# Attention with stationary values in column groups of the array, inside one hybrid decoder layer

## What is computed

```
attn = attend(q, k, v, qi, wi, ki).reshape(B, T, ATTN_DIM)      # 8 heads of 64, top 256 keys of each query
...
logits = jnp.einsum('bqhd,bqkhd->bqhk', q, kg) * (HEAD_DIM ** -0.5)
logits = jnp.where(valid[:, :, None, :], logits, -jnp.inf)
p = jax.nn.softmax(logits, axis=-1)
return jnp.einsum('bqhk,bqkhd->bqhd', p, vg)
...
mixed = jax.nn.sigmoid(ga) * (attn @ w_o_attn) + jax.nn.sigmoid(gc) * (conv_out @ w_o_conv)
h = x + mixed @ w_merge
```

## Time and profile before

| | us |
|---|---|
| median of 3 runs | 1750.7 (1750.21 to 1755.4) |
| span of the profiled execution | 1750.6 |
| PE busy | 1683.5 (96%) |
| DVE busy | 1242.1 (71%) |
| ACT busy | 695.0 (40%) |
| POOL busy | 881.0 (50%) |

### The profile page before, as it was taken

One profiled execution on the slowest core, in us unless ns is written; L12 is line 12 of the kernel. 1 busy time (PEld: TensorE's weight loads), 2 busy tenths in 40 slices (PEclk: granted clock), 3 DMA queues, 4 the chain that ended last, 5 costly groups with the idle time before them and its releaser, 6 DMA issues.

```text
span 1750.6 us, 31893 instructions
## 1 busy us (share of the span) xinstructions
PE 1683.5 (96%) x11519; PEld 1618.8 (92%) x11519; DVE 1242.1 (71%) x1957; ACT 695.0 (40%) x1054; POOL 881.0 (50%) x466
## 2 busy tenths in 40 slices
PE   7999999999999989999799998999999999999999
PEld 5858999999999878889799998999999999999999
DVE  5569999999899645565543378877677776655555
ACT  4755552232111377776212335434444444211110
POOL 2504762455786556664221225766666666733331
PEclk9999999999999889999999999999999999999999
DMA  5321112111776242322343312222222222622222
GB/s 197 84 70 37 36 48 86 61 49 61 267 236 207 75 140 77 87 85 85 110 135 132 143 64 80 88 75 83 72 77 79 72 94 86 231 97 96 96 77 97
DMA packets 66978, 178.32 MB, mean 102 GB/s; under 512 B 15386, under 2 KB 15514, under 8 KB 66762
## 3 DMA queue, kind: packets, MB, share of 16 engines
q1 hardware_dynamic: 56786, 140.91, 24.3%
q10 hardware_dynamic: 9392, 32.10, 4.8%
q0 software_dynamic: 720, 4.29, 0.6%
HBM read 141.79 MB, written 35.58 MB: 101 GB/s over the span
## 4 chain that ended last, share of the span: by engine, by line
PE 76%; DVE 11%; ACT 3%; POOL 3%; issue 3%; SPq 2%; DMA 1%; DVEq 0%; ACTq 0%; POOLq 0%
PE PS L667 17%; PE PS L1079 15%; PE PS L1143 11%; PE PX L1079 6%; PE PS L1002 5%; PE PS L1047 5%; PE PS L955 4%; PE PX L1143 4%; PE PS L925 2%; DVE S L2158 2%; DVE M L2156 2%; PE PX L938 2%; PE PS L983 2%; DVE LD L2138 2%; PE PS L770 1%
## 5 line engine op out<-in xcount | busy, mean ns | idle before, releaser
L667 PE MATMUL PS<-XH,WHI 128*128 128x346 f32 (+1 forms) x984 | 322.1, 327 | 5.8 <-POOL WLO L1778 4.5
L667 PE MATMUL PS<-XL,WHI 128*128 128x346 f32 (+1 forms) x984 | 318.6, 324 | 0.0
L667 PE MATMUL PS<-XH,WLO 128*128 128x346 f32 (+1 forms) x984 | 318.0, 323 | 0.0
L1778 POOL TENSOR_TENSOR WLO<-WRAW,WHI 128x1024 fp32r<-128x1024 f32 x58 | 143.4, 2472 | 296.8 <-ACT WHI L1171 296.7
L2158 DVE MATCH_REPLACE8 S<-M,S 128x1024 f32<-128x1024 f32 (+3 forms) x224 | 206.1, 927 | 0.0
L667 PEld LDWEIGHTS PS<-XH,WHI 128*128 128x128 f32 x984 | 186.9, 190 | 15.7 <-issue 8.8
L2156 DVE MAX8 M<-S 128x8 f32<-128x1024 f32 (+3 forms) x224 | 200.8, 932 | 0.4
L667 PEld LDWEIGHTS PS<-XL,WHI 128*128 128x128 f32 x984 | 187.1, 190 | 0.0
L667 PEld LDWEIGHTS PS<-XH,WLO 128*128 128x128 f32 x984 | 187.1, 190 | 0.0
L2432 DVE TENSOR_TENSOR HY<-HY,PS 128x344 f32<-128x344 f32 x198 | 100.9, 514 | 79.2 <-PE PS L1143 79.2
L1143 PE MATMUL PS<-FH,DLO 128*128 128x344 f32 x396 | 126.7, 320 | 0.0
(11 more groups left out here) (369 smaller groups left out, 4818.5 us busy)
## 6 DMA issues: line engine op xcount, KB each, us to landing
WRAW<-wtiles SPq DMA_DIRECT2D x49, 512.0 KB, 3.7
KR<-cache_k SPq DMA_DIRECT2D x64, 256.0 KB, 3.1
RING<-cache_v SPq DMA_DIRECT2D x64, 256.0 KB, 3.0
ffn_act<-TG ACTq DMA_DIRECT2D x22, 516.0 KB, 2.7
FRAW<-ffn_act SPq DMA_DIRECT2D x11, 1032.0 KB, 7.0
RAWG<-wtiles SPq DMA_DIRECT2D x22, 512.0 KB, 3.7
RAWV<-wtiles SPq DMA_DIRECT2D x22, 512.0 KB, 4.4
DRAW<-wdown SPq DMA_DIRECT2D x11, 1024.0 KB, 4.9
```

Of the source, the lines that this page charges most:

```text
L667: last = nc.tensor.matmul(PS[b][:, c, 0:n], w[b][:, kk, :], x[:, kk, t0 + c * n:t0 + (c + 1) * n], start=(kk == 0 and p == 0), stop=(kk == ...
L1778: nc.gpsimd.tensor_tensor(WLO[b][:, :, :], WRAW[b][:, :, :], WHI[b][:, :, :].bitcast(F32), ALU.subtract).then_inc(w_lo[b], 1)
```

## The change

`pv(u)` now makes the values stationary (64 columns) and the transposed probabilities moving (128 columns). Even key tiles add up on partitions 0 to 63 of `px_out`, odd ones on 64 to 127: two column groups of the array. One more matmul (`px_sum`) spreads the reciprocal row sums over partitions 64 to 127. The result has queries as columns: ACT `half(u)` copies the lower half of PSUM to `HALVES`, DVE `out(u)` adds the upper half and multiplies by the spread reciprocals into `AO`, which already has the layout of `AH`. The reciprocal moves to its own step `recip(u)`. In `attend`, ACT's order is expo(u+2), half(u-1), t_evac(u+1), and DVE's is logits(u+2), recip(u+1), out(u-1).

The decode values are multiplied in plain fp32 without casts: in units 10, 12, 14 and 16 of each head pair, sixteen matmuls (stationary 32 columns of `PZ`, moving 128 columns of `RING`) into four column groups. `value_high` and `value_low` are gone, and SP loads sixteen pages at once, behind unit 16 of the head pair before. `AH` and `AL` of the first three head pairs are made during the last one (`attention_high` on ACT at units 4, 7 and 10, the subtraction on POOL). There are no transposes at the end; the first output tile now runs q=0 before q=1, and ACT casts the weight tile (`hi(1, 21)`) ahead of the last `half`.

```
-                    last = nc.tensor.matmul(px_out[u % 2][0:ROWS[b], :], PTB[u % 2][0:w, kt, 0:ROWS[b]], v,
-                                            start=(kt == 0), stop=(kt == KT_N[b] - 1))
+                pe.wait_ge(a_rc, NU * i + u + 1)
+                    w, g = min(P, S_W[b] - kt * P), HD * (kt % 2)
+                    nc.tensor.matmul(px_out[u % 2][g:g + HD, 0:r], v, PTB[u % 2][0:w, kt, 0:r], start=(kt < 2), stop=(kt >= n - 2))
+                last = nc.tensor.matmul(px_sum[u % 2][HD:P, 0:r], SM[0:r, 36 + u:37 + u].to_broadcast([r, HD]),
+                                        CK[0:r, C_ID:C_ID + r], start=True, stop=True)
...
+                for k in range(4):
+                    for j in range(4):
+                        last = nc.tensor.matmul(px_dec[u % 2][32 * j:32 * j + 32, :], PZ[:, 4 * (i % 2) + k, heads],
+                                                RING[j // 2][:, 4 * (j % 2) + k, cols], start=(k == 0 and i % 2 == 1),
+                                                stop=(k == 3))
...
+            def half(u, i):
+                act.wait_ge(a_pv, NU * i + u + 1 + FREE)
+                nc.scalar.copy(HALVES[u % 2][HD:P, 0:r], px_out[u % 2][0:HD, 0:r]).then_inc(a_hf, 1)
...
             def out(u, i):
-                dve.wait_ge(a_exp, NU * i + u + 1)
-                nc.vector.reciprocal(SM[0:r, 36 + u:37 + u], SM[0:r, 36 + u:37 + u]).then_inc(a_rc, 1)
-                dve.wait_ge(a_pv, NU * i + u + 1 + FREE)
-                ins = nc.vector.tensor_scalar(AT[0:r, b, ds(i * P + e * HD, HD)], px_out[u % 2][0:r, :],
-                                              SM[0:r, 36 + u:37 + u], None, ALU.mult)
+                dve.wait_ge(a_hf, NU * i + u + 1)
+                if KT_N[b] > 1:
+                    nc.vector.tensor_tensor(total, total, px_out[u % 2][HD:P, 0:r], ALU.add).then_inc(a_sum, 1)
+                    dve.wait_ge(a_sum, len(SUMMED) * i + SUMMED.index(u) + 1)
+                ins = nc.vector.tensor_tensor(out, total, px_sum[u % 2][HD:P, 0:r], ALU.mult)
...
-            pe.wait_ge(a_o, 4 * NU + FREE)
-            for t in range(NB):
-                    last = nc.tensor.transpose(at_banks[t % 4][:, j * P:j * P + ROWS[t]], AT[0:ROWS[t], t, j * P:(j + 1) * P],
+            pe.wait_ge(d_o, 2)
+            for j in range(4):
+                for q in range(2):
+                    last = nc.tensor.matmul(PX[0][:, 8 * j + 4 * q:8 * j + 4 * q + 4], OD[q][:, j * P:(j + 1) * P],
```

More of the change, by code:

```diff
@@ L357, in build, with values_part @@
         KLAST_HIGH = max(g for g in range(NS * PAGES) if KSLOT[g] >= 4)
[L359 to L365, removed]
+        VALUES = (10, 12, 14, 16)
+        SPLIT = (4, 7, 10)
+        SUMMED = [x for x, (b, e) in enumerate(UNITS) if KT_N[b] > 1]
+        def values_part(u):
+            return VALUES.index(u) if u in VALUES else None
         FIRST = ("P1", "P2", "P5", "P6", "P3", "P7", "P4")
@@ L972, in decode_values @@
             def decode_values(u, i):
[L975 to L983, removed]
+                part = values_part(u)
+                if part is None:
+                    return None
+                if part == 0:
+                    for b in range(2):
+                        for h in range(2):
+                            pe.wait_ge(ring_in[b][h], 32 * PAGES + 64 * (i + 1))
+                cols, heads = slice(part * P, (part + 1) * P), slice(32 * (i // 2), 32 * (i // 2) + 32)
+                if i % 2 == 0:
+                    for j in range(4):
+                        nc.tensor.matmul(px_dec[u % 2][32 * j:32 * j + 32, :], PTN[:, heads], VT[0:LR, 8, cols], start=True, stop=False)
+                for k in range(4):
+                    for j in range(4):
+                        last = nc.tensor.matmul(px_dec[u % 2][32 * j:32 * j + 32, :], PZ[:, 4 * (i % 2) + k, heads],
+                                                RING[j // 2][:, 4 * (j % 2) + k, cols], start=(k == 0 and i % 2 == 1),
+                                                stop=(k == 3))
                 return last
@@ L995, in _, with out_chunk @@
                 attend(i, i == 3, decode_values)
+            def out_chunk(b, q, c, k0=0, k1=4):
+                xh, xl = ((AH, AL), (COH, COL))[q]
+                for kk in range(k0, k1):
+                    for p, (w, x) in enumerate(((WHI, xh), (WHI, xl), (WLO, xh))):
+                        last = nc.tensor.matmul(PS[q][:, c, 0:CW], w[b][:, 4 * q + kk, :], x[:, kk, C0 + c * CW:C0 + (c + 1) * CW],
+                                                start=(kk == 0 and p == 0), stop=(kk == 3 and p == 2))
+                return last
             def out_part(b, q):
                 for c in range(NCH):
[L999 to L1004, removed]
+                    last = out_chunk(b, q, c)
                 return last
@@ L1917, in _ @@
                 head_low(0, 0, part)
-            for q in range(3):
-                value_low(q, 0)
             attend(0, False)
@@ L2226, in attend @@
                         logits(u + 2, i)
+                    if u + 1 < NU or not last:
+                        recip(u + 1, i)
                     if u >= 1:
                         out(u - 1, i)
[L2229 removed]
+                    elif i > 0:
+                        out(NU - 1, i - 1)
+                    if i == 0 and u == 0:
                         dve.wait_ge(g_last, 16)
[L2231 to L2239 removed]
             def decode_max():
@@ L2530, in _constants @@
             ck[8 * s + h, C_NM + 16 + s] = 0.0
+    for j in range(4):
+        ck[32 * j:32 * j + 32, C_OH + j] = 1.0
+        ck[32 * j + 8 * j:32 * j + 8 * j + 8, C_OH + 4] = 1.0
     ck[0:16, C_ROWP] = 1.0
```

226 lines of the change are left out of this document (98 added, 128 removed).

## The result

The changed kernel takes 1775.2 us in the median of 4 runs (1771.03 to 1777.23), the kernel before, beside it, 1752.6 us (1750.21 to 1755.4). The ratio is 1.0134, 95% interval 1.0112 to 1.0156: 1.3% slower. I had forecast 1742 us, 0.5% faster, with a range from 1719 to 1764.

What follows compares the result with a forecast made beforehand. A closed loop over DVE and ACT, not PE, was to bound the attention: 24.7 + 1.5 + 0.4 = 26.6 us a pass, 213 + 2 + 8 = 223 us (+1); with -9 behind it about 1742 us, range 1719 to 1764.

Steps and rivals of the forecast that it cites:

- the loop I described: Attention, each unit: logits, exponential, ACT's copy, add, multiply, next logits form one closed loop, 24.7 us a pass.
- The two waits that should show it: Attention: DVE waiting for ACT's copy and ACT's exponential for DVE's maximum, together over 100 us.
- Passes are even: Attention: even and odd passes of nearly one length, 26 to 28 us.
- The mean clock: Granted clock between 612 and 836 us: 0.85 to 0.95 expected.
- The rival built on the opposite: Attention: column groups don't run side by side, PE's work is 31.1 us a pass, 1768 us; chance 0.08.
- the rest of the loop: Attention: hand-over to the exponential, copy, add, multiply and two hand-overs, 0.87 us a unit, 7.5 us a pass.
- The waits beyond it: Attention, per pass: 1.5 us ahead of block 8, 0.4 for decode adds, 1 for the clock.
- The tail: Behind the attention: even output row's matmuls done 19.9 us after the last unit's end instead of 28.9, -9 us.
- Clock: Whole attention: waiting engines get a lower clock and PE is the bound again, 1763 us at 0.72; chance 0.15.
- Shorter loop: Attention: no extra wait for block 8 and no loss by the clock, 1722 us; chance 0.17.
- A smaller gain at the end: Behind the attention: last head's copies and the convolution's casts queue on ACT, 4 of 9 us go, 1747; chance 0.10.

Runs made afterwards that it cites:

- e2: Changed kernel with a second copy of the lower half on ScalarE ahead of the real one in each of 72 units: 1785.2 us, ratio 1.0191.
- e3: Changed kernel with each unit's matmul of the sums issued three times instead of once: 1773.2 us, ratio 1.0123 to the kernel before.
- e1: Changed kernel with ScalarE's copy of unit u-1's lower half moved ahead of the exponential of unit u+2: 1729.4 us, ratio 0.9877 to the kernel before.
- e4: As e1, with the scaling of the decode results `OD` moved earlier in the last pass: 1724.6 us, ratio 0.9846 to the kernel before.

## Why the prediction was wrong

**What held.** PE was no longer the bound, and the loop I described closed. The two waits that should show it are 76.0 and 74.1 us, with 11.3 more on `AO`, well over 100. Passes are even, though at 30 to 31 us and not 26 to 28. The mean clock of 0.89 lies in 0.85 to 0.95. Column groups run side by side, as the earlier trace rows had shown: 32 records of decode values in four groups took 1.08 us, and I had taken 1.06. The rival built on the opposite fell with it. The rule on weight loads in the Trainium skill ("TensorE: Matmul & The Clock Gate", Part 3) would have had the groups one behind another, and the trace disagrees; I had passed over that the same part also measures three column tiles at 2.38 times the speed, with which the trace agrees in kind.

**What failed: the rest of the loop, taken as 0.87 us a unit.** It measures 1.10. Term by term, in the turn of the loop shown above:
- exponential's end (678.33 + 0.72) to the copy, 0.12 us where I had 0.04. The read of ACT's accumulator ends at 679.14 (678.96 + 0.18), and this copy, which writes partitions 64 to 127, starts behind it. The read alone doesn't hold the next instruction back: e2's added copy, to partitions 0 to 63, starts while it runs. The read has a row of its own in the view of the earlier trace rows, from which I took the exponential's row alone;
- copy 0.26, as in the earlier trace rows;
- start of the add to start of the multiply 0.33, and from there to the logits 0.32. I had 0.29 each and took off 0.09 for overlap. The multiply waits for the add's semaphore, and the next logits didn't overlap either.

0.23 us in the 68 units from the fifth on are 16 of the 22.9 us by which the attention missed its forecast. A term that is multiplied by 72 was put together from single durations, with the one reduction unproven.

**The waits beyond it: near.** I had 1.5 us for block 8, 0.4 for decode adds and 1 for the clock, 2.9 us a pass. Passes 2 to 7 take 30.55 us in the mean. The exponentials are 7.4 of them as forecast, the logits 10.0 for 9.8, and the loop 9.6 for 7.5 (each less one add for block 0). 3.6 us are left for 2.9. Of these 2.3 stand ahead of block 8's logits: 1.6 in passes at full clock (e3), 2.0 with a decode add, 2.6 at half clock. 0.5 stand ahead of block 0's logits. 1.1 to 1.4 stand ahead of block 4's where the clock is low at the start of a pass and PE has block 8's values and six transposes to do first, and nothing where it is full. Those two places I hadn't looked for. The clock's part, against the same places at full clock, is 4.0 us at block 8 and 5.8 at block 4, 10 us for the 8 charged: the clock was not what the forecast missed.

The account by passes, against the 222.8 us that the terms add up to: pass 1 took 27.4 us for 27.6; passes 2 to 7 took 3.0 more each than 27.6, 17.7 together; and from the start of pass 8 to the last value matmul it took 34.5 us (824.59 to 859.08) for 29.6. That is 22.4 us.

**The tail.** From the end of the last unit's matmuls (859.57) to the even row of output matmuls (880.88) it took 21.3 us for 19.9, so 7.6 us came back of 9; the table above, from the start of the last value matmul to the last output matmul, has 8.0. `OD` took 3.51 us for 3.4. Its 16 records ran at half clock (0.50), 3.58 us for 2. The 72 output matmuls behind them took 14.2 us (866.68 to 880.88) for 14.3, the low clock at their start included, where twelve took 3.60 us; twelve at full clock take 1.91 at the 0.159 us of the later ones. The wait of DVE is the one that the Trainium skill ("SBUF — State Buffer", Who interferes with whom) describes: a DVE instruction with two SBUF inputs contends with a GpSimd instruction that reads SBUF, and the order of issue decides which one is blocked. The traces agree: 2.83 us for the scaling that began behind POOL's subtraction, 0.75 for those that began ahead of it.

**The choice among cases.** With 1.10 in it the sum would have been some 17 us more, 1759: slower by 0.5%, inside the range but on the other side. What I had not asked is how firm the sum was. Before, a pass took 27.8 us, and the 9 us of the tail are 1.1 more of each; my 27.6 left 1.3 us a pass, or 0.14 us a unit, for a chain of six steps and their hand-overs. And I never worked out the edit that opens the loop, though the order of ACT was in front of me; e1's passes of 25.6 us show what was there to be had.

**The rivals.** Clock: no, at 0.89 with PE waiting, and 10 us in all. Shorter loop: no, it was longer. Groups one behind another: no. A smaller gain at the end: 7.6 of 9 us came back. That the result lies on the slower side, outside my range, is the work of the mechanism I had forecast, with a term that was too small.

## To carry to other kernels

When a change gives two engines a new hand-over inside a pipelined unit, write down each engine's order and look for a circle; if there is one, its length per turn is the bound, whatever the engines' loads say, and every 0.1 us in it counts as often as there are units. Then move the late step ahead of the long one on its engine: here one swap turned +1.3% into -1.2% against the kernel before. Price such a circle with start-to-start distances of the trace, and not with durations: a distance holds the hand-overs, the read of the accumulator and the semaphores too.

## What I had not expected of the hardware

- Behind an exponential with row sums stands a read of ACT's accumulator that ends 0.09 us after it (679.14 and 679.05 us). A copy from PSUM to partitions 64 to 127 starts behind the read, 0.12 us after the exponential's end. Copies that write from partition 0 on and have nothing to wait for start within 0.01 us of the exponential's end: e2's added copy, and those to `PTB` in the kernel before. That the partitions are the reason is argued from these rows, not tested.
- The same 16 records of 4 columns (L1024) took 3.58 us in the changed kernel, at a granted clock of 0.50 and behind 3.67 us without work for PE, and 2.32 us in e4, which began at full clock and behind 0.85 us without work.
- A scaling with two SBUF inputs that begins 0.24 or 0.31 us ahead of POOL's subtraction keeps its 0.75 us; the one that begins behind it takes 2.83.
- Two kernels whose attention differs only by one scaling near its end take 207.4 us (e1) and 200.9 (e4) for it, with clocks of 0.94 and 0.97 between 620 and 800 us. Differences of 5 us in one profiled attention shouldn't be read as an effect.
